# Two down units in every turn, a reordered first turn, and a tail of unequal pieces in a float32 transformer kernel

## The reference, cut to what matters

```python
def swiglu(x, w_gu, w_down):
    gate, up = jnp.split(x @ w_gu, 2, axis=-1)
    return (jax.nn.silu(gate) * up) @ w_down
...
h = h + 0.5 * swiglu(rms_norm(h, ffn1_norm[l]), ffn1_w_gu[l], ffn1_w_down[l])
```

## Time and profile before

| what | value |
|---|---|
| median of 3 runs | 3207.75 us (3206.0 to 3209.1) |
| the profiled execution's own time | 3203.08 us |
| its span in the trace | 3201.3 us |
| TensorE (PE) busy | 97% |
| VectorE (DVE) busy | 67% |
| ScalarE (ACT) busy | 38% |
| GpSimd (POOL) busy | 42% |
| DMA queue of SyncE | 28.4% of 16 engines |
| mean granted clock of TensorE | 0.991 |

### The profile page before, as it was taken

How to read it: one execution, slowest core, us unless ns; L and a number is a source line. 1 busy time by engine, 2 the same in 40 slices (tenths; PEclk the granted TensorE clock), 3 DMA queues, 4 the chain that set the end, 5 groups by cost and what they waited for, 6 DMA issues and landing times.

```text
span 3201.3 us, 56181 instructions
## 1 busy us (share of the span) xinstructions
PE 3117.3 (97%) x21236; PEld 2846.7 (89%) x21236; DVE 2143.3 (67%) x3071; ACT 1214.0 (38%) x1825; POOL 1352.8 (42%) x960
## 2 busy tenths in 40 slices
PE   7999999999999999999999999999999999999999
PEld 7999988899999999999998888788888776788998
DVE  7888654476588886888663477533235678668885
ACT  5434443322343344344443322432324444344442
POOL 3444442143544443444442132644465562344443
PEclk9999999999999999999999999999999999999999
DMA  4333322133333333333322133333333533233333
GB/s 134 98 99 99 87 74 60 51 94 118 100 93 96 97 98 87 92 98 99 92 81 67 47 89 120 102 92 109 94 90 94 110 105 117 66 95 97 102 99 96
DMA packets 546214, 299.02 MB, mean 93 GB/s; under 512 B 24368, under 2 KB 529840, under 8 KB 545904
## 3 DMA queue, kind: packets, MB, share of 16 engines
q1 hardware_dynamic: 515728, 259.86, 28.4%
q10 hardware_dynamic: 30304, 36.65, 3.6%
HBM read 278.37 MB, written 16.91 MB: 92 GB/s over the span
## 4 chain that ended last, share of the span: by engine, by line
PE 59%; issue 22%; POOL 8%; DVE 7%; ACT 1%; DMA 1%; ACTq 1%; POOLq 0%; DVEq 0%; SPq 0%
PE aux L790 21%; PE pair L725 21%; PE pair L727 15%; POOL wl L586 8%; DMA raw<-ffn_w_gu 1%; DVE R L1903 1%; DVE tmp L1913 1%; ACTq L1696 0%; DVE al L1918 0%; DVE TL L1909 0%; DVE R L1902 0%; DVE hT L1842 0%; DVE xl L2146 0%; DVE tmp L1818 0%; PE aux L759 0%
## 5 line engine op out<-in xcount | busy, mean ns | idle before, releaser
L586 POOL TENSOR_TENSOR wl<-raw,wh 128x256 fp32r<-128x256 f32 (+3 forms) x848 | 1174.0, 1404 | 1819.0 <-ACT wh L1306 1377.4
L1306 ACT ACTIVATE wh<-raw 128x1024 fp32r<-128x1024 f32 (+4 forms) x613 | 511.6, 835 | 474.0 <-DMA raw<-ffn_w_gu 242.7
L1842 DVE SCALAR_TENSOR_TENSOR hT<-pair,hT 128x528 f32 (+3 forms) x208 | 144.9, 697 | 169.0 <-PE pair L725 127.2
L727 PE MATMUL pair<-xh,wh 128*128 128x264 f32 x1344 | 231.2, 293 | 21.9 <-DVE xl L2146 11.4
L727 PE MATMUL pair<-xl,wh 128*128 128x264 f32 x1344 | 221.4, 287 | 0.0
L725 PE MATMUL pair<-xh,wh 128*128 128x512 f32 x776 | 219.3, 404 | 0.1
L727 PE MATMUL pair<-ah,wh 128*128 128x264 f32 x1256 | 211.7, 286 | 5.0 <-ACT wh L1306 3.5
L727 PE MATMUL pair<-xh,wl 128*128 128x264 f32 x1344 | 214.3, 284 | 1.2 <-POOL wl L586 1.1
L727 PEld LDWEIGHTS pair<-xh,wh 128*128 128x128 f32 x1344 | 187.5, 190 | 29.6 <-issue 14.1
L725 PE MATMUL pair<-xl,wh 128*128 128x512 f32 x776 | 211.4, 394 | 0.0
L725 PE MATMUL pair<-xh,wl 128*128 128x512 f32 x776 | 208.7, 394 | 0.3 <-POOL wl L586 0.3
(11 more groups left out here) (426 smaller groups left out, 6687.8 us busy)
## 6 DMA issues: line engine op xcount, KB each, us to landing
raw<-ffn_w_gu SPq DMA_DIRECT2D x176, 512.0 KB, 3.8
raw<-w_in SPq DMA_DIRECT2D x103, 512.0 KB, 3.8
raw<-ffn_w_down SPq DMA_DIRECT2D x96, 256.0 KB, 2.7
raw<-ffn_w_down SPq DMA_DIRECT2D x32, 384.0 KB, 3.4
raw<-w_out SPq DMA_DIRECT2D x24, 512.0 KB, 3.8
raw<-w_ffn_gate SPq DMA_DIRECT2D x22, 512.0 KB, 4.6
raw<-w_ffn_up SPq DMA_DIRECT2D x22, 512.0 KB, 3.8
gate_scratch<-gst ACTq DMA_DIRECT2D x32, 256.0 KB, 3.0
```

The costliest lines, as they stand in the source:

```text
L586: ins = nc.gpsimd.tensor_tensor(wl[:, k % SPL, n], raw[:, k % SPL, n], wh[:, k % SPL, n].bitcast(F32), ALU.subtract)
L727: mm = nc.tensor.matmul(pp[:, h, 0:th], wk, x[:, kk, t0 + h * th:t0 + (h + 1) * th], start=first, stop=last)
L1306: nc.scalar.activation(wh[:, k % SPL, n0:n], raw[:, k % SPL, n0:n], ACT.Copy).then_inc(S["split_hi"], 1)
L1842: v.scalar_tensor_tensor(halves(hm, T // 2), psum_pair(k, T // 2), factor, halves(hm, T // 2), ALU.mult, ALU.add).then_inc(S["evacuated"], ...
```

## The change

There are three edits, all in `ffn_w` and its helpers, in all four passes.

First, every one of the 18 turns has two down units: turns 0 to 15 those of hidden tiles 0 to 15 (32 units), and turns 16 and 17 four units of hidden tiles 16 to 19, for output tiles 2 to 5. `own_pair` and the paths for fewer down units go away.

Second, the tail is still eight units, but output tiles 2 to 5 have only the two hidden tiles left that were not done: units of 6, 6, 2, 2, 2, 2, 6, 6 tiles (`TAIL_KT`).

Third, in the first turn of a pass TensorE issues the high-weight terms of P1, P2 and P4, and then their low-weight terms.

The diff, cut to its core (the same edit in the loops of the other engines is left out):

```diff
-DOWNS = (2,) * 15 + (1, 1, 0)
-assert len(DOWNS) == W_PAIRS and sum(DOWNS) == 4 * KD
-W_KT = [KD] * (2 * PLAIN) + [x for nd in DOWNS for x in [KD, KD] + [BLOCK] * nd] + [W_TAIL] * KD
+TAIL_KT = (W_TAIL,) * 2 + (W_TAIL - BLOCK,) * 4 + (W_TAIL,) * 2
+W_KT = [KD] * (2 * PLAIN) + [KD, KD, BLOCK, BLOCK] * W_PAIRS + list(TAIL_KT)
...
+                def main(b, w, x):
+                    for t, y in enumerate(x):
+                        for kk in range(4):
+                            nc.tensor.matmul(b[:, 0:th], w[0](kk), y(kk), start=t == 0 and kk == 0, stop=False)
+
+                def rest(b, w, x):
+                    for kk in range(4):
+                        mm = nc.tensor.matmul(b[:, 0:th], w[1](kk), x[0](kk), start=False, stop=kk == 3)
+                    return mm
...
                 pe.wait_ge(S["split_hi"], U(l, k, i) + 1)
-                if own is not None:
-                    pe.wait_ge(S["evacuated"], U(l, k - 1) + 1 + PAIRS)
+                pe.wait_ge(S["w_free"], n + 1)
+                if first:
+                    main(*p1)
+                    main(*p2)
+                    pe.wait_ge(S["w_tlo"], 4 * fs + 4)
+                    pe.wait_ge(S["split_hi"], U(l, k + 1, i) + 1)
+                    main(*p4)
+                    pe.wait_ge(*up_lo)
+                    rest(*p1).then_inc(S["w_prod"], 1)
+                    rest(*p2).then_inc(S["gemm_done"], 1)
+                    pe.wait_ge(*gate_lo)
+                    rest(*p4).then_inc(S["gemm_done"], 1)
                 else:
-                    pe.wait_ge(S["w_free"], n + 1)
...
                 for j in range(2, KD):
-                    gemm(l, k + j, W_TAIL, (ah, al), th)
+                    o = W_TAIL - TAIL_KT[j]
+                    gemm(l, k + j, TAIL_KT[j], (ah[:, o:W_TAIL, :], al[:, o:W_TAIL, :]), th)
```

More of the change, by code:

```diff
@@ L348, in singles @@
         def singles():
[L350 to L353, removed]
+            for t in range(16, W_PAIRS):
+                yield t, W_FIRST + 4 * t, (2 * (t - 16) + 2, 2 * (t - 16) + 3)
         class Plan:
@@ L520, in ffn_w @@
                     load(l, ub + 2 * j + 1, cols(up, l, 0, KD, up0 + j * P), KD)
-                for g in range(1, 4):
+                for g in range(1, 5):
                     k = ub + W_FIRST + 16 * (g - 1)
@@ L531, in ffn_w @@
                     for j, m in enumerate(ms):
[L532 to L536, removed]
+                        load(l, ub + k + 2 + j, cols(down, l, 4 * BLOCK, BLOCK, m * P), BLOCK)
+                for m, kt in enumerate(TAIL_KT):
+                    load(l, ub + W_END + m, cols(down, l, FT - kt, kt, m * P), kt)
             def tiles(l, ub, w, n, kt, c0=0):
@@ L617, in ffn_w @@
                     turn(l, ub + k, n0 + t, 0, len(ms))
-                run(l, ub + W_END, [W_TAIL] * 4, KD // 4)
+                for m, kt in enumerate(TAIL_KT):
+                    split(l, ub + W_END + m, kt)
             def ffn(l, ub, beside):
@@ L769, in norm_sum_2, with turn @@
                 mm.then_inc(S["ss_done"], 1)
-            def turn(l, k, n, i, fs, th, xs, a0, nd=2, own=None):
+            def turn(l, k, n, i, fs, th, xs, a0, first=False):
                 s, s1 = k % SPL, (k + 1) % SPL
@@ L794, in turn @@
+                up_lo, gate_lo = (S["split_done"], U(l, k, i) + 1), (S["split_done"], U(l, k + 1, i) + 1)
                 pe.wait_ge(S["split_hi"], U(l, k, i) + 1)
[L795 to L801 removed]
@@ L841, in block @@
                     return (ah[:, o:o + BLOCK, :], al[:, o:o + BLOCK, :]), fi * FT + BLOCK * (g + 1)
-                for g in range(1, 4):
+                turn(l, ub + W_FIRST, n0, 0, fs, th, *block(0), first=True)
+                with pe.Fori(0, 3) as i:
+                    turn(l, ub + W_FIRST + 4, n0 + 1 + i, i, fs, th, *block(0))
+                for g in range(2, 5):
                     with pe.Fori(0, 4) as i:
@@ L845, in ffn_w @@
                 for t, k, ms in singles():
-                    turn(l, ub + k, n0 + t, 0, fs, th, *block(3), len(ms), own_pair(t, ub))
+                    turn(l, ub + k, n0 + t, 0, fs, th, *block(4))
                 k = ub + W_END
@@ L1355, in activated, with turn @@
                                      ACT.Copy).then_inc(S["ahi_done"], 1)
-            def turn(l, k, n, i, T, f, tile, nd=2, after=2, own=None):
+            def turn(l, k, n, i, T, f, tile, final=False):
                 th = T // 2
-                if own is not None:
-                    act.wait_ge(S["w_read"], n * 2 - 1)
                 act.wait_ge(S["w_prod"], n * 5 + 5 + 1)
[L1363 to L1369, removed]
-                else:
-                    hi(l, q, i, KD * P)
-                    hi(l, q + 1, i, KD * P, HK4)
+                nc.scalar.activation(tm(SQA)[:, 0:th], aux[:, 3, 0:th], ACT.Copy).then_inc(S["w_p1"], 1)
+                hi(l, k + 3, i, BLOCK * P)
+                if final:
+                    hi(l, k + 4, i, TAIL_KT[0] * P)
+                    hi(l, k + 5, i, TAIL_KT[1] * P)
+                else:
+                    hi(l, k + 4, i, KD * P)
+                    hi(l, k + 5, i, KD * P, HK4)
                     w_his(n + 1, 0, n * 5 + 5 + 3)
@@ L1377, in turn @@
                 activated(f, tile, T)
[L1378 to L1379 removed]
+                hi(l, k + 6, i, (TAIL_KT[2] if final else BLOCK) * P)
             def ffn_w(l, ub, fi, T, nrm, gain, last, fs, own):
```

46 lines of the change are left out of this document (15 added, 31 removed).

## The result

| | median | range | runs |
|---|---|---|---|
| before | 3209.1 us | 3201.8 to 3213.8 | 13 |
| changed | 3223.0 us | 3213.5 to 3230.2 | 13 |

The ratio is 1.0043, 95% interval 1.0035 to 1.0051: the changed kernel is 13.9 us slower. The forecast was slower, by 7.5 us. The runs of each kernel spread over 12 and 17 us here, and the two profiled executions lie at opposite ends: 3203.08 us before, 6 us under its median, and 3227.34 us after, 4.3 above. The profiles are 24.2 us apart, of which some 10 belong to that.

The account below looks back on a forecast made before the run. TensorE, busy 97% of the span, was taken as the bound, so time could go only from its waits or half clock. Terms -14.2 - 4.1 + 25.4 + 0.4 = +7.5 us on 3207.75 gave 3215.3 us, range 3206 to 3221.

Parts of the forecast that it names:

- the term for turns 1 to 16: Turns between first and last: moved down units and VectorE's added reads cost nothing; zero.
- Last turn (-14.2): Last turn of each pass: a second down unit covers the wait for VectorE's read; all idle time gone, -14.2 us.
- First turn (-4.1): First turn of each pass: high terms first shorten waits, 0.3 us in A and B, 1.8 in C, 1.7 in D.
- Tail of A, B and C (+25.4): Tail: VectorE's 3.35 us chain from add to add outlasts 1.45 us units; 8.5 us a pass, +25.4 in three.
- GpSimd's stretch: Tail of A, B, C: GpSimd's split slows a VectorE instruction; 0.55 us in one link, 0.3 in two more, 1.15 a pass.
- Tail of D (+0.4): Tail of D, without `prep`: unit 6 waits for unit 2's slot to be reloaded; +0.4 us, bounds 0 and 1.5.
- second rival: Clock falls to half in the tails; up to 1.7 us a pass more, +12.6 in all, 3220.4; chance 0.15.
- fourth and fifth rivals: Fourth: tail links 2.4 us or less, 3201, chance 0.08; fifth: half the last turn's waits stay, 3222, chance 0.05.

Follow-up runs that it names:

- three-loop kernel: Changed kernel with turns 12 to 15 written out on all engines instead of in a fourth loop; 1.0023 of before, 1.0011 when run again.
- kernel with two loops: Changed kernel with turns 8 to 17 all written out, leaving two loops a pass on every engine; 1.0031 of before.
- short units at both ends: Changed kernel with the two-tile tail units of A, B and C at output tiles 0, 1, 6, 7 instead of 2 to 5; 0.9990 of before.
- `prep` late: Changed kernel with VectorE adding unit m before `prep` of m - 1 in the tails of A, B and C, squares in two buffers; 1.0004 of before.
- the pairs: Changed kernel with turns 12 to 15 written out, short tail units alternating with long, VectorE's adds and `prep` mostly in pairs (A, B, C); 0.9955 of before.

## Why the prediction was wrong

**Where it failed.** The step that failed is the term for turns 1 to 16, which was put at zero: turns 15 and 16 and `own_pair` were put "under the same answer: work moved, no wait either way", and that turns 12 to 14, formerly written out, now run in a loop was not weighed at all. Kernels that differ in this alone stand 6.4 and 10.6 us (one pair, timed twice) and 9 us apart (6.1, 6.2 and 5.7 by medians). Without it, in the three-loop kernel, +7.4 and +3.5 us were measured, where the sum says +7.5. That this comes so near is in part luck: the first turns gave 8.7 us and not 4.1. With the terms as the runs and the profiles give them (-14.2, -8.7, +26.4, +0.8) the sum is +4.3, and with the 6 to 11 us on top +10 to +15, where +13.9 was measured. The range reached to 3221 because every rival was a cost of the tail or of the last turn.

**What the profiles show of that term.** The wait that grows is for VectorE's last read (L1942, L1950 before): 8.3 us in the changed kernel against 2.8. Over all profiles it is 2.1 to 5.2 us (mean 3.7) in the seven with three loops on every engine and 3.1 to 9.8 (mean 6.3) in the six with four. These ranges overlap. Most of it follows turns 4, 8 and 12, the first of a loop or, in turn 12 of a kernel with three, of the written-out part. Turn 8 of pass A starts at 198.3 us and was 18.10 us long. The weights of the turn after it (`ffn_w_gu`, up and gate) land late, and VectorE stands still for them:

```profile
201.81 1.92 SPq L477 DMA_DIRECT2D raw<-ffn_w_gu  x2
```

```profile
210.29 0.69 DVE L1874 TENSOR_TENSOR gst<-raw 128x512 f32<-128x512 f32 x1 [3.73 <-DMA raw<-ffn_w_gu]
...
226.72 0.69 DVE L1874 TENSOR_TENSOR gst<-raw 128x512 f32<-128x512 f32 x1 [2.05 <-DMA raw<-ffn_w_gu]
```

From the issue to VectorE's first sum it is 8.5 us here and 6.8 in the next turn (219.90 to 226.72). The DMA view of 205 to 213 us, in slices of 0.2 us, shows what stands beside the late load: a fetch of instructions at 207.0 us, on q8, and from 207.6 us on the load's end at 8 to 44 GB/s (the fetch on q14, at 211.5 us, comes too late for it):

```profile
GB/s 105 100 154 125 195 248 312 307 300 356 184 115 44 23 23 10 8 10 72 136 187 300 346 259 74 23 20 0 0 0 0 0 41 0 0 0 0 0 0 0
...
q8 instruction: 1, 0.02, 0.7%
q14 instruction: 1, 0.01, 0.4%
```

In the records of all 16 profiles, passes A to C, turns 1 to 14, about 90 turns have such a fetch 6.9 to 9.0 us after their start, and they are 0.7 us longer than 16.03 on the mean; the 580 others, with a fetch at another time or none, 0.1. The bounds of 6.9 and 9.0 were chosen with the turns in view. The changed kernel has 7 and 8 such turns in its two profiles, the three-loop kernel 4 and 5. That is an association in the records, and it carries 1 to 2 of the 6 to 11 us. No run moved a fetch and nothing else. So it is shown that the fourth loop costs in these kernels, and that late gate loads are where some of it is spent. What in the loop costs stays open. One rival was not tried: that it is not the loop but where the code's blocks come to lie, and with them the fetches. The kernel with two loops, slower than the one with three, speaks for it.

**Last turn (-14.2): right.** All four take 16.03 us (15.69 in D) at clock 1.00 without a wait, the length of a turn with one down unit plus 2.9. A and D are shown above.

**First turn (-4.1): right for the profile, too small for the median.** -4.2 in the windows; waits of 1.2 and 0.4 in A against the 1.2 and 0.7 worked out, and then 0.2 for the activation. The half clock comes more often than the earlier trace rows showed, so the edit alone was worth 8.7 us (5.5 to 11.9).

**Tail of A, B and C (+25.4): right.** From 372.07 the fourth short unit could have ended at 377.9; the long one starts at 386.63: 8.8 us, forecast 8.5. Of it GpSimd's stretch is 1.4 (three times 0.5), not 0.55 + 0.3 + 0.3: the overlap does not shift from link to link. The Trainium skill, GPSIMD Engine Reference, 8. Key points, names two inputs from SBUF as what makes a VectorE instruction contend with GpSimd. The trace agrees: L1825, which has two, is stretched, and the add, which reads PSUM, keeps its 0.70 us under a split (385.78). That L1825 escapes when it starts before the split (385.10), my estimate did not have. That the chain and not the units sets the price is shown by three kernels: short units at both ends, `prep` late, and the pairs.

**Tail of D (+0.4): too small.** 0.8 us, in waits of 0.6 and 0.2; with alternating sizes last turn and tail are 1.0 us shorter.

**Rivals.** The clock did fall in one tail of the first profile (B, 0.89), and last turn and tail there were 0.2 us longer than in A and C: the slow units filled the waits. It is commoner than that profile says. In the seven profiles of kernels whose tails in A, B and C are the changed kernel's, it fell in 14 of 21. Twelve times it cost some 0.5 us at most. Twice it fell later, over the first long unit instead of the short ones, and last turn and tail took 50.7 us instead of 48.5. The first row is the tail of B in the changed kernel, the second that of A with the fourth loop on TensorE alone:

```profile
1236.00:1245.00 9.00, 6.22 (x26) 5.41 (x24) 6.33 (x9) 3.58 (x6) 2.83 (x3) 0.50 0.35 102
...
386.60:392.00 5.40, 5.36 (x26) 5.38 (x27) 2.83 (x5) 4.06 (x6) 3.25 (x2) 0.54 0.33 94
```

So the second rival's mechanism is real, its 0.15 was too low, and its price of up to 1.7 us a pass is near the measured one only where the clock falls late. The Trainium skill, TensorE: Matmul & The Clock Gate, A second HAM failure mode: psum-queue depth-cycling, describes such swings for short pauses between groups of matmuls. The trace agrees, with 14 of 21 tails. The fourth and fifth rivals did not happen.

## What to carry to other kernels

When work is taken from a stage, ask what else ran under it: VectorE's chain, at 3.35 us a tile, was free under units of 4.35 and cost 8.8 us a pass under four units of 1.45. The same units in another order, with the chain's work in pairs, cost under 1 us. And a loop in place of written-out code is an edit of its own, worth 6 to 11 us here: try the kernel with and without it before you explain the time by the work. Cost each stage from two executions where a clock level or a load decides it, since one profile can be lucky in several places at once.

## What the hardware showed that I had not expected

Executions of the kernel before spread by 12 us, of the changed one by 17 (0.4 and 0.5%). A first turn with one wait of 2.4 us ran at full clock in one execution (8.55 us) and at half clock, 0.83 on the mean, in another (10.06). With the wait split into 1.2 and 0.4, none of 53 first turns fell. A VectorE instruction with two inputs from SBUF that starts behind GpSimd's split is held back (2.43 us instead of 0.7 at 386.44 with `prep` late), and one that starts 0.16 us ahead of the split is not (0.76 at 385.10). And a fetch of instructions beside the load of a turn's weights goes with 0.7 us more in a turn of 16 us on the mean, up to 2.1.
